# Six raw buffers instead of four for the expert weight units, the two new ones in the space of the stored residual rows

## The reference

```python
h = rms_norm(x, g2)                                  # both groups: 768 tokens
aff = softmax(h @ w_router); gate, idx = top_k(aff.T, cap)   # 16 experts, 32 + 64 tokens each
def expert(wg, wu, wd, ix, g):                       # wg, wu: 1024 x 2816, wd: 2816 x 1024, float32
    xe = h[ix]                                       # 96 rows
    return ((silu(xe @ wg) * (xe @ wu)) @ wd) * g[:, None]
y = x + scatter_add(ye, idx)
```

## Time and profile before

| | us |
|---|---|
| median of 3 runs | 2207.47 (2193.83 to 2209.68) |
| the profiled execution's own time | 2186.04 |
| its span, first to last instruction | 2184.2 |
| TensorE busy in the span | 2122.7 (97%) |
| VectorE, ScalarE, GpSimd busy | 1570.7, 1359.3, 232.9 |
| first product of expert 0 starts | 654.69 |
| read from and written to HBM | 609.70 MB, 13.63 MB |

### The profile page before, as it was taken

The page is one execution under the profiler, slowest core; times in us unless marked ns, Lnnn a source line. Parts: engine busy times, 40 slices in busy tenths (PEclk is TensorE's granted clock), DMA queues, the critical chain, the costliest instruction groups (busy, mean ns, idle before and its releaser), DMA issues.

```text
span 2184.2 us, 27119 instructions
## 1 busy us (share of the span) xinstructions
PE 2122.7 (97%) x10388; PEld 1580.5 (72%) x10388; DVE 1570.7 (72%) x1203; ACT 1359.3 (62%) x1069; POOL 232.9 (11%) x138
## 2 busy tenths in 40 slices
PE   8999999999959999999999999999999999999997
PEld 6858878887846776777677777767767777777765
DVE  5384452234458887888888888888888888798885
ACT  5273362223226777777777777777777777767764
POOL 2102210000120101010110101001010101101010
PEclk9999999999979999999999999999999999999998
DMA  6202131132328999999999999999999999999994
GB/s 235 77 18 105 55 122 58 61 132 71 152 104 325 368 388 363 379 370 377 375 369 377 375 380 371 367 384 366 376 372 381 372 370 388 366 374 375 375 367 184
DMA packets 71916, 623.96 MB, mean 286 GB/s; under 512 B 8352, under 2 KB 8480, under 8 KB 19264
## 3 DMA queue, kind: packets, MB, share of 16 engines
q1 hardware_dynamic: 64128, 595.70, 70.5%
q0 software_dynamic: 7744, 27.67, 4.4%
HBM read 609.70 MB, written 13.63 MB: 285 GB/s over the span
## 4 chain that ended last, share of the span: by engine, by line
PE 84%; DVE 6%; DMA 6%; ACT 3%; issue 1%; POOL 0%; SPq 0%; ACTq 0%; DVEq 0%; POOLq 0%
PE PS L543 26%; PE PS L545 25%; PE PS L544 25%; DMA x_w_raw<-in_w_expert_gate 4%; DVE x_w_low L1187 3%; ACT x_w_high L1117 2%; PE PS L652 2%; PE PS L898 1%; PE PS L635 1%; DMA x_w_raw<-in_w_expert_up 1%; PE PS L666 1%; PE PS L552 1%; DMA w_raw<-in_w_in 1%; PE PS L842 1%; PE PS L763 0%
## 5 line engine op out<-in xcount | busy, mean ns | idle before, releaser
L1187 DVE TENSOR_TENSOR x_w_low<-x_w_raw,x_w_high 128x3072 fp32r<-128x3072 f32 x383 | 1177.9, 3087 | 234.2 <-ACT x_w_high L1117 232.1
L1117 ACT ACTIVATE x_w_high<-x_w_raw 128x3072 fp32r<-128x3072 f32 (+1 forms) x384 | 980.3, 2558 | 259.7 <-PE PS L545 197.7
L543 PE MATMUL PS<-x_w_high,xT_high 128*96 128x512 f32 (+1 forms) x1536 | 580.0, 378 | 4.9 <-DVE x_w_low L1187 4.8
L545 PE MATMUL PS<-x_w_high,xT_low 128*96 128x512 f32 (+1 forms) x1536 | 575.1, 374 | 0.0
L544 PE MATMUL PS<-x_w_low,xT_high 128*96 128x512 f32 (+1 forms) x1536 | 573.2, 373 | 0.0
L543 PEld LDWEIGHTS PS<-x_w_high,xT_high 128*96 128x96 f32 x1536 | 248.1, 162 | 98.8 <-DVE x_w_low L1187 13.3
L545 PEld LDWEIGHTS PS<-x_w_high,xT_low 128*96 128x96 f32 x1536 | 248.0, 161 | 90.1
L544 PEld LDWEIGHTS PS<-x_w_low,xT_high 128*96 128x96 f32 x1536 | 248.6, 162 | 85.7
L543 PE MATMUL PS<-x_w_high,hidden_high 128*96 128x512 f32 x704 | 281.2, 399 | 0.0
L545 PE MATMUL PS<-x_w_high,hidden_low 128*96 128x512 f32 x704 | 276.6, 393 | 0.0
L544 PE MATMUL PS<-x_w_low,hidden_high 128*96 128x512 f32 x704 | 275.8, 392 | 0.0
(11 more groups left out here) (189 smaller groups left out, 1703.3 us busy)
## 6 DMA issues: line engine op xcount, KB each, us to landing
x_w_raw<-in_w_expert_gate SPq DMA_DIRECT2D x96, 1536.0 KB, 8.5
x_w_raw<-in_w_expert_up SPq DMA_DIRECT2D x96, 1536.0 KB, 8.8
x_w_raw<-in_w_expert_down SPq DMA_DIRECT2D x96, 1536.0 KB, 8.5
x_w_raw<-in_w_expert_gate SPq DMA_DIRECT2D x32, 1024.0 KB, 7.3
x_w_raw<-in_w_expert_up SPq DMA_DIRECT2D x32, 1024.0 KB, 7.3
x_w_raw<-in_w_expert_down SPq DMA_DIRECT2D x32, 1024.0 KB, 7.1
w_raw<-in_w_in SPq DMA_DIRECT2D x19, 1024.0 KB, 4.8
x<-in_x_sample SPq DMA_DIRECT2D x8, 512.0 KB, 11.5
```

The lines of the kernel that those rows point to most:

```text
L543: mm(out, sh, mh, start=first, stop=False)
L545: return mm(out, sl, mh, start=False, stop=last)
L1117: a_(xh[:, w % SPLITS, 0:n], xraw[:, w % RAWS, 0:n], ACT.Copy).then_inc(x_high, 1)
L1187: return v.tensor_tensor(out, src, high.bitcast(F32), ALU.subtract)
```

## The change

`RAWS` goes from 4 to 6. Raw buffers 4 and 5 take the 6144 columns at offset 960, where `x` was. The high, low and raw slots are now tensors of their own instead of slices of one. Since 24 units are a multiple of both 4 and 6, a unit's buffer number is still the same in every expert. SyncE's issue of unit w now waits for the split of unit w-6. At unit 4 (the first to use a new buffer) SyncE also waits until all six residual tiles have been stored, which is true for good after the first time. `x_split` gets 3 at the start as before, and 3 instead of 1 after the first top round.

```diff
-RAWS, SPLITS = 4, 3
+RAWS, SPLITS = 6, 3
...
-        xraw = at("x_w_raw", 31680, RAWS * XUNIT).rearrange("p (b n) -> p b n", b=RAWS)
+        xraw = [at(f"x_w_raw{i}", off, XUNIT) for i, off in enumerate((31680, 34752, 37824, 40896, 960, 4032))]
...
                     sp.wait_ge(x_split, e * NXU + w + 1)
+                    if w == 4:
+                        sp.wait_ge(S("x", "residual_stored"), 16 * NT)
                     b = w % RAWS
-                    sp.dma_start(xraw[:, b, 0:unit_width(w)], unit_source(e, w)).then_inc(x_loaded[b], 16)
+                    sp.dma_start(xraw[b][:, 0:unit_width(w)], unit_source(e, w)).then_inc(x_loaded[b], 16)
...
-            dve.sem_inc(x_split, RAWS - 1)
+            dve.sem_inc(x_split, 3)
...
-                    dve.sem_inc(x_split, 1)
+                    dve.sem_inc(x_split, RAWS - 3)
```

More of the change, by code:

```diff
@@ L195, in encoder @@
         cumT = at("cumT", 51008, 512, E)
-        xl = at("x_w_low", 7104, SPLITS * XUNIT, dt=F32R).rearrange("p (b n) -> p b n", b=SPLITS)
-        xh = at("x_w_high", 16320, SPLITS * XUNIT, dt=F32R).rearrange("p (b n) -> p b n", b=SPLITS)
+        xl = [at(f"x_w_low{i}", 7104 + i * XUNIT, XUNIT, dt=F32R) for i in range(SPLITS)]
+        xh = [at(f"x_w_high{i}", 16320 + i * XUNIT, XUNIT, dt=F32R) for i in range(SPLITS)]
         xTh = at("xT_high", 25536, KD * CAP, dt=F32R)
@@ L495, in _ @@
             pool.wait_ge(x_high, 1)
-            nc.gpsimd.tensor_tensor(xl[:, 0, 0:n], xraw[:, 0, 0:n], xh[:, 0, 0:n].bitcast(F32), ALU.subtract
+            nc.gpsimd.tensor_tensor(xl[0][:, 0:n], xraw[0][:, 0:n], xh[0][:, 0:n].bitcast(F32), ALU.subtract
                                     ).then_inc(x_split, 1)
@@ L862, in _ @@
                         f0, nf = DT[q][c]
-                        uh, ul = (a[:, b, 0:nf * D].rearrange("p (f d) -> p f d", f=nf) for a in (xh, xl))
+                        uh, ul = (a[b][:, 0:nf * D].rearrange("p (f d) -> p f d", f=nf) for a in (xh, xl))
                         last_round = [r for r, (r0, rn) in enumerate(HR[q]) if r0 < f0 + nf][-1]
@@ L875, in _ @@
                         k0, nk = KT[q][c]
-                        uh, ul = (a[:, b, 0:unit_width(w)].rearrange("p (k f) -> p k f", k=nk) for a in (xh, xl))
+                        uh, ul = (a[b][:, 0:unit_width(w)].rearrange("p (k f) -> p k f", k=nk) for a in (xh, xl))
                         if kind == "gate" and c == 0 and q > 0:
@@ L1116, in unit_high @@
                 n = unit_width(w)
-                a_(xh[:, w % SPLITS, 0:n], xraw[:, w % RAWS, 0:n], ACT.Copy).then_inc(x_high, 1)
+                a_(xh[w % SPLITS][:, 0:n], xraw[w % RAWS][:, 0:n], ACT.Copy).then_inc(x_high, 1)
             out_done(act, NT - 1, 1)
@@ L1544, in unit_low @@
                 dve.wait_ge(x_high, e * NXU + w + 1)
-                low(xl[:, w % SPLITS, 0:n], xraw[:, w % RAWS, 0:n], xh[:, w % SPLITS, 0:n]).then_inc(x_split, 1)
+                low(xl[w % SPLITS][:, 0:n], xraw[w % RAWS][:, 0:n], xh[w % SPLITS][:, 0:n]).then_inc(x_split, 1)
             def misc_low(what, j, n, n_high, bank):
```

## The result

The changed kernel takes 2177.81 us (median of 19 runs, 2175.12 to 2195.59), the kernel before 2192.55 us in as many runs (2186.05 to 2209.68). The ratio is 0.9936, 95% interval 0.9910 to 0.9962. The profiled execution took 2177.72 us (span 2175.9), against 2186.04 before.

What follows compares the result with a forecast made beforehand. TensorE and transfers were both taken as near their limits, with late loads stalling TensorE. Buffers -9.2 and loop start +0.5 made a gain of 8.7 us: 2207.5 - 8.7 = 2198.8 us, range 2181 to 2213.

Steps and rivals of the forecast that it cites:

- against the median: 2207.5 - 8.7: Whole kernel: the profiled execution's gain of 8.7 us taken off the median of the runs shown, giving 2198.8 us.
- Rival A: Expert loop: unprofiled runs hold more lateness of loads, which six buffers recover, up to 30.1 us, time 2177.4; chance 22%.
- More buffers: minus 9.2 us: Expert loop: earlier loads remove TensorE's stalls, bringing experts from 94.51 to 93.93 us apart; -9.2 us over sixteen experts.
- The bound of 18.1: Expert loop: TensorE's waits for low halves, 13.3 and 4.8 us, as the most that more buffers could recover.
- An advance of 7.8 covers every one of the 52: Expert loop: loads start up to 7.8 us sooner, covering all 52 ScalarE waits for weight loads, longest 2.5 us.
- the transfer engines have the capacity: Expert loop: transfers can build up the advance, narrowly, their busy share rising from 0.96 to 0.966.
- SyncE's added wait: 0: Unit 4 of each expert: SyncE's wait for the stored residual tiles costs nothing, 0 us.
- The start of the loop: +0.5 us: Before the first product: earlier weight loads meet gather 0 and delay it, between 0 and 8.0 us, taken as 0.5.
- Other edits: 0: Slots as separate tensors give the same instructions on the same shapes; 0 us.
- B: Expert loop: transfers bound the usual run, only the head start of units 5 and 6 counts, 7.1 us, time 2200.4; 11%.
- C: Expert loop: lateness comes from rounding and subtracting behind three slots, so stalls stay, time 2208.0; chance 11%.
- D: Loop start: loads under way throughout gather 0 make it take 12.3 us, starting the loop 8.0 later; slower, chance 6%.

Runs made afterwards that it cites:

- experiment 8: Changed kernel, first branch weights' load issued only after the last value windows of the neighbourhood attention landed: 2175.77 us, ratio 0.9915 to the kernel before.
- experiment 1: Changed kernel with its six buffers, but loads issued four places ahead as before the change: ratio 1.0011 to the kernel before, upper-clock median 2188.0 us.
- experiment 4: Changed kernel, units 0 to 6 of the first expert issued as there, all later loads four places ahead: ratio 0.9994 to the kernel before.
- experiment 11: Kernel before (four buffers), branch weights loaded only after the last value windows landed: median 2187.1 us, ratio 0.9945.
- experiment 2: Changed kernel with loads issued five places ahead instead of six: ratio 0.9941 to the kernel before, upper-clock median 2176.9 us.
- experiment 3: Changed kernel, first 12 units of expert 0 issued four places ahead, so no head start: ratio 0.9948 to the kernel before.
- experiment 5: Kernel before (four buffers), only three quarters of each unit loaded from expert 1 on, engine work the same: ratio 0.9949, upper-clock median 2176.5 us.
- experiment 9: Changed kernel with TensorE's idle router time filled with unused products: ratio 0.9960 to the kernel before; 3 of 12 runs near 2177 us.
- experiment 12: Changed kernel with two spare 0.5 MB copies issued ahead of the last four window loads: ratio 0.9999 to the kernel before, runs 2195.99 to 2198.94 us.
- experiment 6: Kernel before without indirect transfers in the loop (only gathers 0 and 1, no results added to the output): ratio 0.9888, median 2167.5 us.

## Why the prediction was wrong

The direction and the mechanism were right; the time, 2198.8 with a range down to 2181, was 21 us too high. Of these, 15.0 are the base (2207.5 against 2192.55) and 6.0 the gain (8.7 against a difference of medians of 14.7). Of the 6.0, 2.9 are a gain forecast too small (11.6 between the groups' medians at the upper clock); the rest comes of where the medians fall in the groups.

**The step that failed is the sum's last one, "against the median: 2207.5 - 8.7".** The median was of three runs, two of them of the group whose profiles show the half clock in the attention (experiment 8), and the gain was taken from an execution without it. The prediction said that no row tells where the others spent the difference, and then used their median as the base all the same. Over 19 runs the base is 2192.55, and the changed kernel's median falls among the runs at clock 0.990: 2177.81. Against the profiled execution the sum, 2177.3, met the changed kernel's own, 2177.72. That it is so close is in part luck: the start term of 0.5 wasn't there, and a delay of 1.4 us from ahead of the router, which nobody forecast, was. Rival A took the 21.4 us for lateness of loads, and its time, 2177.4, came true by luck. Most was clock: 2208.4 - 2188.4 = 20.0 between the groups, and six buffers recovered only 14.0 - 11.6 = 2.4 us more in one than in the other.

**"More buffers: minus 9.2 us" was right for the profiled pair, and mis-sized for the runs.** From first to last y_rows the loop took 1417.6 us and takes 1409.1, 8.5 less in 15 periods against 8.6 forecast. But the execution of before was among its fastest: its 2186.04 is below all 19 runs. The loops of experiments 1, 4 and 11, with four places of advance, lost 11.1, 12.4 and 12.2 us over 15 x 93.94. The gain between runs of one clock is 11.6. The bound of 18.1 wasn't reached; in the runs the term was some 12.

**"An advance of 7.8 covers every one of the 52" held**, and 3.9 us more would have (experiment 2). That the transfer engines have the capacity was right; they are 0.95 busy, where 0.966 was forecast. The way of a load grew by 1.1 us at most: the medians are 8.5 to 9.0 us instead of 8.5 to 8.8 for units of 3 blocks, 7.7 to 8.4 instead of 7.1 to 7.3 for those of 2. The Trainium skill's 358 GB/s for one core ("DMA: Bandwidth & Descriptors", section Specifications) isn't a limit here. The table gives it as a stack's 716 GB/s divided by two cores, and this program runs on one. With the queue full the engines moved 423 GB/s from 638 to 644, and 371 over the loop.

**"SyncE's added wait: 0" held:** units 3, 4 and 5 go out within 2.3 us, with one wait of 0.6 us for the last residual tile among them. **"The start of the loop: +0.5 us" was nothing:** gather 0 took 4.2 us, 4.3 before. Unit 6 was issued at 639.04, as foreseen (637.5 and the 1.4 us by which the execution was late), but the engines moved 423 GB/s from 638 to 644 and not the estimate's 370, so it had landed at 648.3, before the gather was issued at 648.46. **"Other edits: 0" held** (experiment 1).

**Rivals.** B fell in experiments 3 and 4, C in experiment 5. D's mechanism didn't occur. A was right that runs differ more than the profile shows, and mostly wrong in what they differ by.

## What to carry to other kernels

When two resources are both above 0.95 busy, one unit of extra advance can turn all remaining stalls into reserve; compare the mean period of a loop with that of a pass without stalls to see what that is worth, and do so in more than one execution. Before a gain read from one execution is set against a median, find out whether the runs form groups, and compare within a group. A wait of two microseconds on TensorE can cost far more than its length when the clock falls after it, so a transfer that TensorE is about to need shouldn't share the engines with one that is needed later.

## What the runs showed of the hardware that wasn't expected

- In four profiled executions (experiments 2, 4, 9 and 12) the granted clock fell to 0.50 (1.2 GHz) during, or up to 1.2 us behind, a wait of TensorE of 1.9 to 4.4 us between small products, and stayed there for some 34 to 38 us; the runs of that group take 17 us or more longer. In the ten others, with waits of 0 to 2.0 us, it held.
- Beside the window loads from memory, a load of 1 MB took 18.9 us; issued behind their landing, in experiment 8, 5.1 us at most.
- Gather and scatters, 96 rows of 4 KB each way beside 34.6 MB of weights in an expert, are what makes weight loads late (experiment 6, together with 5): a gather takes 12 us from issue to landing beside them and 4.2 without.
